# Head norms of a hybrid encoder step: products with 128 rows, eight products ahead of the sums, and a store that is awaited one stage later

## The reference, cut to what matters

```
# in _gdn: q and k are divided by the root of their sum of squares over 64 channels
q = _l2norm(q.reshape(B, L, GDN_H, GDN_DK)) * (GDN_DK ** -0.5)
k = _l2norm(k.reshape(B, L, GDN_H, GDN_DK))
...
o, S = _gated_delta(q, k, v, g, beta, S0)          # S is an output: new_gdn_s
o = _rmsnorm(o.astype(xqkv.dtype), norm_g) * jax.nn.silu(xg.reshape(B, L, GDN_H, GDN_DV))
# in _diff
o = _rmsnorm(o, sub_g, eps=1e-5) * (1.0 - lam_init)
```

## Time and profile before

| | |
|---|---|
| median of 3 runs | 4042.75 us |
| profiled execution | 4038.68 us |
| its span, first to last instruction | 4036.9 us |
| TensorE busy | 3700.2 us, 92% of the span |
| VectorE busy | 2071.0 us, 51% |
| ScalarE busy | 991.7 us, 25% |
| GpSimd busy | 884.6 us, 22% |
| mean granted TensorE clock | 0.927 |

### The profile page before, as it was taken

The page is one execution under the profiler, slowest core; times in us unless marked ns, Lnnn a source line. Parts: engine busy times, 40 slices in busy tenths (PEclk is TensorE's granted clock), DMA queues, the critical chain, the costliest instruction groups (busy, mean ns, idle before and its releaser), DMA issues. The chain is left out here.

```text
span 4036.9 us, 52162 instructions
## 1 busy us (share of the span) xinstructions
PE 3700.2 (92%) x21292; PEld 3392.2 (84%) x21292; DVE 2071.0 (51%) x3608; ACT 991.7 (25%) x1802; POOL 884.6 (22%) x758
## 2 busy tenths in 40 slices
PE   6888989799899999999987889888989999999997
PEld 5767876599699999999976678656978999999996
DVE  7464432254345565565655653423534555556556
ACT  3233232232321111111233322423323211111112
POOL 2211110011142222222332111101113332222322
PEclk9999997599799999999998999966988999999998
DMA  6521230100111111111163211201001111111112
GB/s 219 155 78 56 66 100 36 64 1 2 33 41 42 43 42 43 42 42 42 36 186 102 87 51 66 83 36 64 1 19 32 41 43 37 48 42 37 44 41 72
DMA packets 121408, 233.60 MB, mean 58 GB/s; under 512 B 34340, under 2 KB 82980, under 8 KB 117768
## 3 DMA queue, kind: packets, MB, share of 16 engines
q1 hardware_dynamic: 121160, 230.18, 18.3%
HBM read 175.58 MB, written 54.18 MB: 57 GB/s over the span
## 5 line engine op out<-in xcount | busy, mean ns | idle before, releaser
L261 PE MATMUL PS<-h_split,w_split 128*128 128x384 f32 x3072 | 1068.8, 348 | 22.2 <-PEq L199 8.3
L263 PE MATMUL PS<-h_split,w_split 128*128 128x384 f32 x3072 | 1045.5, 340 | 0.0
L262 PE MATMUL PS<-h_split,w_split 128*128 128x384 f32 x3072 | 1041.8, 339 | 0.0
L256 POOL TENSOR_TENSOR w_split<-w_full,w_split 128x1024 fp32r<-128x1024 f32 x194 | 472.0, 2433 | 1042.4 <-ACT w_split L248 1042.3
L261 PEld LDWEIGHTS PS<-h_split,w_split 128*128 128x128 f32 x3072 | 587.7, 191 | 45.7 <-issue 28.4
L262 PEld LDWEIGHTS PS<-h_split,w_split 128*128 128x128 f32 x3072 | 584.1, 190 | 1.8
L263 PEld LDWEIGHTS PS<-h_split,w_split 128*128 128x128 f32 x3072 | 583.8, 190 | 0.0
L248 ACT CAST w_split<-w_full 128x1024 fp32r<-128x1024 f32 x194 | 201.8, 1051 | 1317.4 <-PE PS L263 1181.2
L2202 DVE TENSOR_TENSOR x<-x,PS 128x384 f32<-128x384 f32 x528 | 285.6, 552 | 177.4 <-PE PS L263 175.8
L261 PE MATMUL PS<-ffn_act,w_split 128*128 128x384 f32 x1056 | 367.2, 348 | 8.2 <-POOL w_split L256 7.1
L262 PE MATMUL PS<-ffn_act,w_split 128*128 128x384 f32 x1056 | 356.7, 338 | 0.0
(11 more groups left out here) (377 smaller groups left out, 5652.0 us busy)
## 6 DMA issues: line engine op xcount, KB each, us to landing
w_full<-in_w_up SPq DMA_DIRECT2D x88, 512.0 KB, 3.6
w_full<-in_w_down SPq DMA_DIRECT2D x44, 512.0 KB, 3.6
w_full<-in_w_in SPq DMA_DIRECT2D x38, 512.0 KB, 3.7
kq_keep<-split_rows SPq DMA_DIRECT2D x128, 128.0 KB, 2.5
kq_row<-kq_keep SPq DMA_DIRECT2D x32, 512.0 KB, 4.5
x<-x_keep SPq DMA_DIRECT2D x2, 4608.0 KB, 14.3
w_full<-in_w_out SPq DMA_DIRECT2D x16, 512.0 KB, 3.6
gdn_y<-y_keep SPq DMA_DIRECT2D x2, 3456.0 KB, 12.4
```

Source lines behind the costliest of these rows:

```text
L256: pool.tensor_tensor(ws[:, n % SSLOTS, 1, 0:w], wf[:, n % WSLOTS, 0:w], ws[:, n % SSLOTS, 0, 0:w].bitcast(F32), ALU.subtract).then_inc(w_l ...
L261: pe.matmul(out, w_hi, a_hi, start=first, stop=False)
L262: pe.matmul(out, w_hi, a_lo, start=False, stop=False)
L263: return pe.matmul(out, w_lo, a_hi, start=False, stop=last)
```

## The change

Five edits:

1. `head_inv` gets all 128 partitions. GpSimd clears it at the stage's start, and ScalarE's first copy into it waits for that (`rows_zero`). The 8 live rows are written as before.
2. The spreading products read 128 rows of `head_inv` and of the constant `head_get` in place of 8. Rows 8 to 127 of `head_inv` are zero, so the result is the same.
3. At the stage's start TensorE issues 8 products of two constants (`busy_product`, 128 rows, 256 columns, f32) into bank 3 of PSUM, ahead of the first sums. Nothing reads what they write.
4. The states' four stores count on a semaphore that outlives the stage (`states_out`), and `gdn_mix_stage` no longer waits for it.
5. The wait for `states_out` stands at the end of `gather_sgu`, in the stage behind.

```
         inv = at("head_inv", [P, NB, BLK], R(27))            # was [8, NB, BLK]
...
+        def busy_product(pe, out, w=256):
+            pe.matmul(out[:, 0:w], C("ident"), cst[:, CC["upto"][0]:CC["upto"][0] + w], start=True, stop=True)
...
+                @block.gpsimd
+                def _(pool):
+                    pool.memset(inv[:, :, :], 0.0).then_inc(rows_zero, 1)
...
                         act.wait_ge(turned, b + 1)
+                        if b == 0:
+                            act.wait_ge(rows_zero, 1)
                         act.copy(inv[0:rows, b, :], PS[0:rows, 3, 0:BLK]).then_inc(row_done, 1)
...
                 def _(pe):
+                    for _ in range(8):
+                        busy_product(pe, PS[:, 3, :])
+
                     def sums(b):
...
-                            pe.matmul(PS[:, 4 + u % BACK, 0:BLK], K8("head_get", rows, n * P, (n + 1) * P),
-                                      inv[0:rows, b, :], start=True, stop=True).then_inc(back_ready, 1)
+                            pe.matmul(PS[:, 4 + u % BACK, 0:BLK], K8("head_get", P, n * P, (n + 1) * P),
+                                      inv[:, b, :], start=True, stop=True).then_inc(back_ready, 1)
...
-                        sp.dma_start(d["o_gs_s"][l, rows], Sb[rows, :, :, 64 * r:64 * r + 64]).then_inc(s_out, 16)
-                    sp.wait_ge(s_out, 64)
+                        sp.dma_start(d["o_gs_s"][l, rows], Sb[rows, :, :, 64 * r:64 * r + 64]).then_inc(states_out, 16)
                     sp.wait_ge(x_moved, 16)
                     sp.wait_ge(y_moved, 32)
...
                 sp.wait_ge(kept_out, 48)
+                sp.wait_ge(states_out, 64)
```

More of the change, by code:

```diff
@@ L174, in build @@
         PS = top.enter_context(nc.psum_tensor("PS", [P, 8, 512], F32))
-        keep_names = ("w_in0", "w_in1", "w_hi", "w_lo", "x_moved", "kept_out", "out_done", "y_moved")
+        keep_names = ("w_in0", "w_in1", "w_hi", "w_lo", "x_moved", "kept_out", "out_done", "y_moved", "states_out")
         lsem = [top.enter_context(nc.semaphore(n)) for n in keep_names]
-        w_loaded, (w_hid, w_lod, x_moved, kept_out, out_done, y_moved) = lsem[0:2], lsem[2:]
+        w_loaded, (w_hid, w_lod, x_moved, kept_out, out_done, y_moved, states_out) = lsem[0:2], lsem[2:]
         def C(name):
@@ L946, in head_norm_stage @@
             sq = at("head_sq", [P, SLOTS, BLK], R(24))
-            inv = at("head_inv", [8, NB, BLK], R(27))
+            inv = at("head_inv", [P, NB, BLK], R(27))
             col = at("head_col", [P, TT, 8], R(28))
@@ L950, in head_norm_stage @@
             with stage("sq_ready", "sum_ready", "back_ready", "norm_done", "head_link", "recip_done", "root_done",
-                       "turned", "row_done", "silu_done", "eps_done") as (
+                       "turned", "row_done", "silu_done", "rows_zero") as (
                     block, (sq_ready, sum_ready, back_ready, norm_done, lnk, recip_done, root_done, turned, row_done,
-                            silu_done, eps_done)):
+                            silu_done, rows_zero)):
                 gates = [g for _, _, g in parts if g is not None]
@@ L1454, in gdn_mix_stage @@
                      "inc_ready", "sol_done", "wT_ready", "wT_done", "ws_ready", "ws_copied", "ws_turned", "vn_done",
-                     "st_ready", "st_done", "o_ready", "o_done", "ktm_ready", "s_out", "gdn_link")
+                     "st_ready", "st_done", "o_ready", "o_done", "ktm_ready", "gdn_link")
             with stage(*names) as (block, sems):
@@ L1459, in gdn_mix_stage @@
                  n0_done, nt_ready, nt_done, n_ready, n_done, inc_ready, sol_done, wT_ready, wT_done, ws_ready,
-                 ws_copied, ws_turned, vn_done, st_ready, st_done, o_ready, o_done, ktm_ready, s_out, lnk) = sems
+                 ws_copied, ws_turned, vn_done, st_ready, st_done, o_ready, o_done, ktm_ready, lnk) = sems
                 def levels(t):
@@ L1500, in _ @@
                         rows = slice(64 * r, 64 * r + 64)
-                        sp.dma_start(d["o_gs_p"][l, rows], S[rows, 0, :, 64 * r:64 * r + 64]).then_inc(s_out, 16)
+                        sp.dma_start(d["o_gs_p"][l, rows], S[rows, 0, :, 64 * r:64 * r + 64]).then_inc(states_out, 16)
                     sp.wait_ge(st_done, 2 * PT_TILES + 1)
```

## The result

The changed kernel takes 4009.89 us, the median of 4 executions (3996.78 to 4015.11), against 4043.23 us of the kernel before (4042.28 to 4045.03): a ratio of 0.9914, 95% interval 0.9895 to 0.9933, 33 us faster. That is the forecast direction and 1.8 times the forecast size (-18.8 us); the median lies just under the lower end of the range. A repeat beside the parts of the change gave 4000.2 us against 4039.75, a ratio of 0.9899 (0.9884 to 0.9914). The profiled execution took 4014.65 us.

A forecast was written before the change was run, and what follows sets the result against it. Bound by head norms on TensorE at clock 0.50 and SyncE's store wait: -3.3 us per first, -2.6 per second head norm, twice each -11.8, with stores -18.8, from 4042.75 to 4024 us; range 4010 to 4044.

The forecast's parts named there:

- The bound: Both head norms hang on TensorE's list at clock 0.50; SyncE waits 3.5 us for states ending each delta-rule stage.
- The store, -7.0 us: End of the delta-rule stage: without SyncE's wait the next stage begins 3.5 us sooner, twice, -7.0 us.
- Rows raise the clock: Spreading products of the head norms: 128 rows raise the clock, -5.3 us in a first head norm, -4.6 in a second.
- the rival of the zero rows: Head norms: zero rows don't count for the clock, only the added products raise it; +1.0 us, 4043.8 us; chance 0.18.
- the third sums' share: Head norms, sums after the first spreading block: start at the high clock, keep it 2.1 us, -2.0 us.
- The eight products, +4.0 us: Start of each head norm: the added constant products delay the first sums by 4.0 us, between +3.4 and +5.0.
- the slower rival: Head norms: the constants don't raise the clock, +5.0 us at four places; +13.0 us, 4055.8 us; chance 0.07.
- the mixed one: Head norms: added products fail to raise the clock but the 128-row blocks do; 4036 us; chance 0.09.
- The sums behind them, -2.0 us: Head norms, first sums after the added products: start at the high clock, lose it after 2.1 us; 0 to -3.1.
- The stages behind, 0 with 1 us each: Stages after the edited ones: may meet the clock elsewhere in its course; 0, within 1 us at four places.
- The rival of the clock kept throughout (3992 us): Head norms: wide products between the sums keep the clock high, about -11 us per stage; 3992 us; chance 0.06.

## Why the prediction was right or wrong, point by point

- **The bound: right.** The head norms' end hangs on TensorE's list, at the low clock, and SyncE's wait held up the next stage. Every gain that could be placed came from these two.
- **The store, -7.0 us: right.** -6.7 us by the traces, -6.9 by the time. The wait behind `o_sgu` is hidden by the barrier.
- **Rows raise the clock: right, and the rival of the zero rows wrong.** -5.3 and -4.6 us were forecast, -6.3 and -5.6 measured with the rows alone. The rule of the Trainium skill that I set beside it ("TensorE: Matmul & The Clock Gate", "What's actually happening": the monitor goes by how busy the PE has been) doesn't tell these cases apart: with 8, 32 and 64 rows TensorE was as busy as with 128, and the clock stayed at 0.50. Too small was the third sums' share: I gave them 2.1 us of the high clock, they kept it to their end, 2.6 to 2.9 us, in every trace with 128 rows and nothing put among them; and the first block of a first head norm took 4.7 us in place of 5.4, where I had taken 0.25 us off.
- **The eight products, +4.0 us: right in size.** They put the sums off by 4.4 us in the first head norm (a start 6.24 us into the stage against 1.81) and 3.8 us in the second. The constants do raise the clock, so the slower rival and the mixed one fall.
- **The sums behind them, -2.0 us: the step that failed.** I bounded it by 3.3 us of high clock from one place where narrow products had lost it, and took that as the most there could be. In the first head norms they kept it for 2.6 us (-2.6), in the second for all 5.3 us (-5.0), outside the bound. The trace of the kernel before had a second such fall, in layer 1, which I didn't use: there the products of 16 columns lost the clock after 1.0 us. One kind of work with 1.0 and 3.3 us in one trace was a sign that neither was a limit. So the products cost 1.8 us in one head norm and gave 1.3 us in the other, +1.1 us in four stages and not +8.0. This is 7 of the 12 us by which the edited places beat the forecast (-30.7 against -18.8 us); the rows are 4.1 of the rest, and 1.2 us show only where rows and products stand together.
- **The stages behind, 0 with 1 us each: too tight.** The delta rule lost 2.9 us in layer 1 and 0.4 in layer 2 between the first two traces, the long stage being one in which the clock fell early, and everything else moves by some 13 us between traces. The spread of the changed kernel's times (18 us) against the 3 us of the first four executions of the kernel before looked like an effect of the change; over more executions the kernel before had 4034 to 4052 us itself.
- **The rival of the clock kept throughout (3992 us): wrong.** The clock falls in each head norm at least once.

Open is what decides when the clock falls under narrow products: whether the sums keep it for 2.6 or 5.3 us, and whether the delta rule's products of 16 columns keep it for 1 or 3 us.

## What to carry to other kernels

Where TensorE is busy and its granted clock is still 0.50, look at the rows of the contraction in its wide products: padding them from 8 to 128 rows with zeros cost no time on the engine here and gave 24 us for a memset beside other work. Rows alone were not enough: the first sums have 128 rows and 8 moving columns, and with the rows alone they still ran 10.3 us at 0.50. The products of constants that only raise the clock were paid ahead of the work here and returned about as much; measure the real products at full rows without it first. And when one fall of the clock is all the trace has, it is a sample and not a bound: the same sums kept the clock for 2.6 us in one stage and for all of their 5.3 us in another.

## What the runs showed of the hardware that I had not expected

- Products of 384 columns with 64 rows left the clock at 0.50 through twelve blocks of 5.1 us (head norms 40.7 and 38.2 us), just as 8 and 32 rows did; with 128 rows, 120 of them zero, it rose within the first block in the rows-only kernel. The time of such an instruction was the same, 5.49 us for eight of them at the low clock, at 8, 32, 64 and 128 rows.
- Sums of 8 moving columns ran at 0.11 us an instruction for 5.3 us on end at a clock of 1.00, 48 of them, though 128 x 16 products had lost it after 3.3 us, and after 1.0 us in layer 1 of the same trace.
